# Head norms between the projection chunks, side columns as the stationary operand, and one routing pass for both token tiles

## The reference

```python
def mixer_inputs(h, w_in, q_norm, k_norm, rope):          # first block, x and ctx
    qa, ka, va, fb, qc, kc, vc = jnp.split(h @ w_in, points, axis=-1)
    qa = rms_norm(qa.reshape(b, l, 6, 64), q_norm)
    ka = rms_norm(ka.reshape(b, l, 2, 64), k_norm)
    if rope is not None:                                  # only for x
        qa, ka, qc, kc = (apply_rope(v, cos, sin) for v in (qa, ka, qc, kc))
...
# even layer: h @ ev_w_in has 3072 columns in twelve chunks and 8 more, dt, one for each head
# odd layer: q (8 heads), ksl and kwn (2 heads each) get rms_norm and rope, and then NSA
# experts:
logits = t @ router                                       # 256 x 8
top_val, top_idx = lax.top_k(logits, 2)
gates = sum(one_hot(top_idx) * softmax(top_val))
```

## Time and profile before

| | us |
|---|---|
| median of 3 runs | 2687.01 (2672.03, 2687.01 and 2688.66) |
| profiled execution | 2674.17 |
| its span | 2671.4 |
| PE busy | 2401.7 |
| DVE busy | 1760.9 |
| ACT busy | 1321.8 |
| POOL busy | 201.2 |

### The profile page before, as it was taken

How to read it: one execution, slowest core, us unless ns; L and a number is a source line. 1 busy time by engine, 2 the same in 40 slices (tenths; PEclk the granted TensorE clock), 3 DMA queues, 4 the chain that set the end, 5 groups by cost and what they waited for, 6 DMA issues and landing times. The chain is left out here.

```text
span 2671.4 us, 44765 instructions
## 1 busy us (share of the span) xinstructions
PE 2401.7 (90%) x17271; PEld 2182.7 (82%) x17271; DVE 1760.9 (66%) x2845; ACT 1321.8 (49%) x2069; POOL 201.2 (8%) x200
## 2 busy tenths in 40 slices
PE   7888999889986989979789986676999999999998
PEld 5777898679876879979689986466999999999997
DVE  3645555555555555565555553656999999999997
ACT  2343443434342544432344441224777777777776
POOL 0500000000005000007100005000000000000000
PEclk9988999989998989989689997887999999999999
DMA  8614555155633045534035541023999999999995
GB/s 340 235 50 174 190 214 205 67 208 219 232 134 111 17 163 190 185 119 142 1 121 187 190 185 66 1 87 136 354 346 334 334 345 340 330 346 337 331 351 212
DMA packets 82228, 542.86 MB, mean 203 GB/s; under 512 B 9328, under 2 KB 9840, under 8 KB 33904
## 3 DMA queue, kind: packets, MB, share of 16 engines
q1 hardware_dynamic: 79184, 529.57, 53.4%
q10 hardware_dynamic: 2848, 10.55, 1.1%
HBM read 539.03 MB, written 1.05 MB: 202 GB/s over the span
## 5 line engine op out<-in xcount | busy, mean ns | idle before, releaser
L847 PE MATMUL bank<-w_hi,src_hi 128*128 128x256 f32 x2304 | 657.3, 285 | 14.2 <-DVE src_lo L618 4.6
L2922 DVE TENSOR_TENSOR w_lo<-ring,w_hi 128x1024 fp32r<-128x1024 f32 x528 | 636.7, 1221 | 44.9 <-ACT w_hi L2851 32.8
L848 PE MATMUL bank<-w_lo,src_hi 128*128 128x256 f32 x2304 | 650.6, 282 | 0.0
L849 PE MATMUL bank<-w_hi,src_lo 128*128 128x256 f32 x2304 | 649.2, 282 | 0.0
L847 PEld LDWEIGHTS bank<-w_hi,src_hi 128*128 128x128 f32 x2304 | 438.7, 190 | 32.2 <-issue 23.7
L848 PEld LDWEIGHTS bank<-w_lo,src_hi 128*128 128x128 f32 x2304 | 439.1, 191 | 6.8
L849 PEld LDWEIGHTS bank<-w_hi,src_lo 128*128 128x128 f32 x2304 | 440.0, 191 | 0.0
L847 PE MATMUL bank<-src_hi,w_hi 128*128 128x256 f32 x1472 | 427.2, 290 | 12.7 <-DVE w_lo L1154 8.9
L1154 DVE TENSOR_TENSOR w_lo<-ring,w_hi 128x1024 fp32r<-128x1024 f32 x264 | 322.9, 1223 | 170.1 <-ACT w_hi L1091 170.0
L848 PE MATMUL bank<-src_lo,w_hi 128*128 128x256 f32 x1472 | 422.2, 287 | 0.0
L849 PE MATMUL bank<-src_hi,w_lo 128*128 128x256 f32 x1472 | 421.9, 287 | 0.0
(11 more groups left out here) (410 smaller groups left out, 2837.7 us busy)
## 6 DMA issues: line engine op xcount, KB each, us to landing
ring<-in_moe SPq DMA_DIRECT2D x176, 1024.0 KB, 7.2
ring<-in_ffn SPq DMA_DIRECT2D x66, 1536.0 KB, 6.5
ring<-in_moe SPq DMA_DIRECT2D x176, 512.0 KB, 6.8
ring<-in_ffn_ev SPq DMA_DIRECT2D x22, 1536.0 KB, 6.6
oT<-in_w_ada SPq DMA_DIRECT2D x20, 1024.0 KB, 6.1
big<-in_w_ada SPq DMA_DIRECT2D x20, 1024.0 KB, 8.3
ring<-in_w_in SPq DMA_DIRECT2D x18, 1024.0 KB, 6.7
ring<-in_w_out SPq DMA_DIRECT2D x12, 1024.0 KB, 4.9
```

What stands on the lines that cost most here:

```text
L847: pe.matmul(out, ah, bh, start=start and i == 0, stop=False, skip_group_check=True)
L848: pe.matmul(out, ah, bl, start=False, stop=False, skip_group_check=True)
L849: mm = pe.matmul(out, al, bh, start=False, stop=stop and i == n - 1, skip_group_check=True)
L2922: dve.tensor_tensor(wl, piece, wh.bitcast(F32), ALU.subtract).then_inc(p.w_lo[kind].sem, 1)
```

## The change

- `side_product` swaps its operands: the eight columns are stationary and all 256 tokens stream past, 24 matmuls in place of 48. The result lies on eight partitions; DVE copies it to SBUF (`side_keep`) and PE turns it with two small transposes (`side_turn`). In the even projection the product stands behind chunk 9 of 0 to 11 and the turn behind chunk 10, in banks 6 and 7, so that the chunks have three pairs of banks in place of four.
- First block: POOL norms and turns the A heads of `x` during the projection of `x` itself, when two chunks are taken (and, in layer 0, the small loads have landed). During the context's projection it turns only the C heads (`x_turns1`) and then computes the power for the context's norms.
- `ctx_heads1` has no Block any more. It is `inline`: DVE issues the squares and sums of the context's heads after chunk 1 (chunk 0 in layer 1), and the scaling and gains after the next chunk.
- Odd layer: all norms and turns move from POOL to DVE, between chunks 1 to 5 (`nsa_norms`). POOL keeps the two powers.
- `route` handles both token tiles in each instruction where it can, and releases PE's counting before it computes the weights.

```diff
-def side_product(p, pe):
-
-    for m in range(NT):
-        ms = slice(m * P, m * P + P)
-        mm = products(pe, p.ps[0][:, m * NE:m * NE + NE],
-                      [((p.srcH[:, k, ms], p.srcL[:, k, ms]), (p.sideH[:, k, :], p.sideL[:, k, :]))
-                       for k in range(KT)], True, True)
-    return mm
+def side_product(p, pe, bank):
+
+    mm = products(pe, bank[0:NE, 0:T],
+                  [((p.sideH[:, k, :], p.sideL[:, k, :]), (p.srcH[:, k, :], p.srcL[:, k, :])) for k in range(KT)],
+                  True, True)
+    mm.then_inc(p.sig("side_ready").sem, 1)
+
+
+def side_keep(p, dve, bank):
+
+    dve.wait_ge(*p.sig("side_ready")(1))
+    dve.tensor_copy(p.work[0:NE, 2560:2560 + T], bank[0:NE, 0:T]).then_inc(p.sig("side_kept").sem, 1)
+
+
+def side_turn(p, pe, bank):
+
+    pe.wait_ge(*p.sig("side_kept")(1))
+    for t in range(NT):
+        mm = pe.transpose(bank[:, t * NE:t * NE + NE], p.work[0:NE, 2560 + t * P:2560 + t * P + P], p.ident[0:NE, 0:NE])
+    mm.then_inc(p.sig("side_turned").sem, 1)
...
-    pairs_of_banks = 3 if riders or gate is not None else 4
+    pairs_of_banks = 3 if riders or gate is not None or side is not None else 4
...
+                    if side is not None and c == n - 3:
+                        pe.wait_ge(*sided(1))
+                        side_product(p, pe, p.ps[6])
+                    if side is not None and c == n - 2:
+                        side_turn(p, pe, p.ps[7])
...
-            if side is not None:
-                pe.wait_ge(*taken(n))
-                pe.wait_ge(*sided(1))
-                side_product(p, pe).then_inc(ready.sem, 1)
...
+                if side is not None and c == n - 3:
+                    side_keep(p, dve, p.ps[6])
+                if inline is not None:
+                    inline(dve, chain, c)
...
             if side is not None:
-                dve.wait_ge(*ready(n + 1))
-                dve.tensor_copy(side, p.ps[0][:, 0:NT * NE].rearrange("p (m n) -> p m n", m=NT)).then_inc(taken.sem, 1)
-    ready.passed(total)
-    taken.passed(total)
+                dve.wait_ge(*p.sig("side_turned")(1))
+                dve.tensor_copy(side, p.ps[7][:, 0:NT * NE].rearrange("p (m n) -> p m n", m=NT))
...
-def x_heads1(p, proj, l):
+def square_sums(p, chain, dve, src, junk, st):
+
+    parts, tiles, heads, n = src.shape
+    sq = junk[:, 0:tiles * heads * n].rearrange("p (t h d) -> p t h d", t=tiles, h=heads)
+    chain(dve.tensor_tensor(sq, src, src, ALU.mult))
+    chain(dve.tensor_reduce(st.rearrange("p (t h) -> p t h", t=tiles), sq, AX_X, ALU.add))
+
+
+def mean_squares(p, dve, st, n):
+
+    dve.tensor_scalar(st, st, 1.0 / n, EPS, ALU.mult, ALU.add).then_inc(p.meansq.sem, 1)
+
+
+def scale_heads(chain, dve, src, st):
+
+    parts, tiles, heads, n = src.shape
+    chain(dve.tensor_tensor(src, src, st.rearrange("p (t h) -> p t h", t=tiles).unsqueeze(3)
+                            .broadcast_to([parts, tiles, heads, n]), ALU.mult))
+
+
+def gain_heads(chain, dve, src, gain):
+
+    parts, tiles, heads, n = src.shape
+    chain(dve.tensor_tensor(src, src, gain.unsqueeze(1).unsqueeze(1).broadcast_to([parts, tiles, heads, n]), ALU.mult))
+
+
+def x_heads1(p, proj, l, loads):

     def beside(pool, taken):
         chain, junk = pool_chain(p, pool), p.big[:, 0:2048]
-        norm_rows(p, chain, pool, heads_of(proj, 0, 8), [(0, 6, p.row(ROWS1, "q_norm", l, HD)),
-                                                         (6, 2, p.row(ROWS1, "k_norm", l, HD))], junk, True)
-        for a in (0, 896):
-            rope_rows(chain, pool, heads_of(proj, a, 8), p.con_at(CON1, "rope_c", NT), p.con_at(CON1, "rope_s", NT),
-                      junk)
+        if loads:
+            pool.wait_ge(*p.sig("small_loaded")(16 * len(loads)))
+        pool.wait_ge(*taken(2))
+        src = heads_of(proj, 0, 8)
+        norm_rows(p, chain, pool, src, [(0, 6, p.row(ROWS1, "q_norm", l, HD)), (6, 2, p.row(ROWS1, "k_norm", l, HD))],
+                  junk, True)
+        rope_rows(chain, pool, src, p.con_at(CON1, "rope_c", NT), p.con_at(CON1, "rope_s", NT), junk)
     return beside


+def x_turns1(p, proj, queries):
+
+    def beside(pool, taken):
+        rope_rows(pool_chain(p, pool), pool, heads_of(proj, 896, 8), p.con_at(CON1, "rope_c", NT),
+                  p.con_at(CON1, "rope_s", NT), p.big[:, 0:2048])
+        rsqrts(p, pool, [16 if queries else 4])
+    return beside
+
+
 def ctx_heads1(p, proj, l, queries):

-    gains = [(0, 6, p.row(ROWS1, "q_norm", l, HD)), (6, 2, p.row(ROWS1, "k_norm", l, HD))]
     src = heads_of(proj, 0, 8) if queries else heads_of(proj, 6 * HD, 2)
-    with p.nc.Block(no_gpsimd_drain=True) as block:
-        @block.gpsimd
-        def _(pool):
-            rsqrts(p, pool, [16 if queries else 4])
-
-        @block.vector
-        def _(dve):
...
+    def inline(dve, chain, c):
+        if c == first:
+            square_sums(p, chain, dve, src, p.work[:, 0:1024], st)
+            mean_squares(p, dve, st, HD)
+        if c == first + 1:
+            rsqrt(p, dve, st)
+            scale_heads(chain, dve, src, st)
+            if queries:
+                gain_heads(chain, dve, src[:, :, 0:6, :], p.row(ROWS1, "q_norm", l, HD))
+            gain_heads(chain, dve, src[:, :, src.shape[2] - 2:, :], p.row(ROWS1, "k_norm", l, HD))
+    return inline


...
         linear(p, Normed(x, p.scl[:, 0, 0, :], mod(l, 0, 0)), 6, out=px, loads=second_loads if l == 0 else (),
-               riders=riders(0, (0, 0, 2, 2, 4, 4)) if l == 0 else ())
+               beside=x_heads1(p, px, l, second_loads if l == 0 else ()), riders=riders(0, (0, 0, 2, 2, 4, 4)) if l == 0 else ())
         ctx_src = Normed(ctx, p.scl[:, 0, 1, :], mod(l, 0, 1))
         if l == 0:
-            linear(p, ctx_src, 6, out=pc, beside=x_heads1(p, px, l), riders=riders(6, (0, 0, 2, 2, 4, 4)),
-                   after=norm_scales(p, l, (1,)))
+            linear(p, ctx_src, 6, out=pc, beside=x_turns1(p, px, True), riders=riders(6, (0, 0, 2, 2, 4, 4)),
+                   after=norm_scales(p, l, (1,)), inline=ctx_heads1(p, pc, l, True))
         else:
-            linear(p, ctx_src, 3, out=pc, out_at=[256, 512, 1280], beside=x_heads1(p, px, l))
-        ctx_heads1(p, pc, l, l == 0)
+            linear(p, ctx_src, 3, out=pc, out_at=[256, 512, 1280], beside=x_turns1(p, px, False),
+                   inline=ctx_heads1(p, pc, l, False))
         block1_attention(p, px, l, True)
...
-            norm_rows(p, chain, pool, v, [(0, n, gain)], junk, True)
-            rope_rows(chain, pool, v, p.con_at(CON2, "rope_c", NT), p.con_at(CON2, "rope_s", NT), junk)
+        rsqrts(p, pool, [16, 8])
     return beside
+
+
+def nsa_norms(p):
+
+    queries = heads_of(p.proj, 0, 8)
+    keys = [heads_of(p.proj, 768 + 256 * w, 2) for w in range(2)]
+    st = p.small[:, 0:16]
+    cos, sin = p.con_at(CON2, "rope_c", NT), p.con_at(CON2, "rope_s", NT)
+
+    def inline(dve, chain, c):
+        if c == 1:
+            square_sums(p, chain, dve, queries, p.work[:, 0:1024], st)
+            mean_squares(p, dve, st, HD)
+        if c == 2:
+            rsqrt(p, dve, st)
+            scale_heads(chain, dve, queries, st)
+        if c == 3:
+            gain_heads(chain, dve, queries, p.row(ROWS2, "nsa_q"))
+        if c in (3, 4):
+            square_sums(p, chain, dve, keys[c - 3], p.work[:, 0:256], st[:, 4 * (c - 3):4 * (c - 3) + 4])
+        if c == 4:
+            mean_squares(p, dve, st[:, 0:8], HD)
+            rope_rows(chain, dve, queries, cos, sin, p.work[:, 512:2560])
+        if c == 5:
+            rsqrt(p, dve, st)
+            for w in range(2):
+                scale_heads(chain, dve, keys[w], st[:, 4 * w:4 * w + 4])
+                gain_heads(chain, dve, keys[w], p.row(ROWS2, "nsa_k", 1 + w, HD))
+                rope_rows(chain, dve, keys[w], cos, sin, p.work[:, 512:1024])
+    return inline
...
-            side_product(p, pe).then_inc(logit.sem, 1)
+            side_product(p, pe, p.ps[0])
+            side_turn(p, pe, p.ps[2])
             pe.wait_ge(*chosen(1))
...
-            chain(dve.tensor_copy(logits, p.ps[0][:, 0:16].rearrange("p (t e) -> p t e", t=NT)))
+            side_keep(p, dve, p.ps[0])
+            dve.wait_ge(*p.sig("side_turned")(1))
+            chain(dve.tensor_copy(logits, p.ps[2][:, 0:16].rearrange("p (t e) -> p t e", t=NT)))
             for t in range(NT):
...
+            dve.tensor_tensor(first, lanes, at[:, :, 0:1].broadcast_to([P, NT, NE]), ALU.is_equal)
+            chain(dve.tensor_tensor(second, lanes, at[:, :, 1:2].broadcast_to([P, NT, NE]), ALU.is_equal))
+            dve.tensor_tensor(hot, first, second, ALU.add).then_inc(chosen.sem, 1)
+            dve.wait_ge(*ex(1))
...
-    linear(p, Normed(p.x, p.col("od_mix")), 7, out=p.proj[:, :, 0:O_COLS], beside=nsa_heads(p), loads=[
+    linear(p, Normed(p.x, p.col("od_mix")), 7, out=p.proj[:, :, 0:O_COLS], beside=nsa_heads(p), inline=nsa_norms(p), loads=[
```

74 lines of the change are left out of this document (39 added, 35 removed).

## The result

The changed kernel took **2647.36 us** (median of 4 runs, 2645.13 to 2650.41), the kernel before 2686.99 (2672.03 to 2688.66) on the same chip: a ratio of the means of **0.9865** with a 95% interval of 0.9828 to 0.9903, or some 36 us less (the medians lie 39.6 apart). The forecast was 2640, between 2619 and 2661. A second set of runs gave 0.9864 (2644.27).

What follows compares the result with a forecast made beforehand. TensorE, busy 90% of the span, was taken as the bound, so only its standstills count: 9.0 + 6.9 + 5.0 + 9.9 + 7.8 = 38.6, plus 2 for the clock, 40.6 off the mean 2680.5 gives 2640 us, range 2619 to 2661.

Steps and rivals of the forecast that it cites:

- layer 0, x and context: First block, layer 0: the Block between the context's projection and the attention goes, 9.0 us less (7.5 to 10).
- layer 1, x and context: First block, layer 1: x 3.8 us longer, context to attention 10.7 shorter, together 6.9 us less (6.0 to 7.5).
- even projection: Even layer: side product and turn move between chunks, saving 8.4 us behind them, net 5.0 us less (4.0 to 5.6).
- odd projection: Odd layer's norms on DVE: NSA begins at 1633.3 in place of 1643.2, 9.9 us less (9 to 12).
- route: Router product 3.6 us less, instructions from logits to PE's release 4.3 less; 7.8 in all (6.8 to 9.0).
- Contention: POOL beside x's projection stretches w_lo by 1.1 to 1.6 us, within 3.4 of slack; zero counted, at most 1.5 lost.
- Layer 1's wait: POOL works 26.2 us after chunk 1 of x in layer 1, so the context's front begins 3.8 us later.
- The clock: Shorter holes let PE's clock stay up in some places behind them; 2 us counted.
- Rival 1: The clock stays up behind the shortened holes: gain 46 to 55 us, about 2630 us; chance 0.11.
- Rival 2: Chunks pay through late POOL work beside x and waits at inline norms: gain 18 to 34, about 2655; chance 0.11.
- Rival 3: Savings aren't carried on, as later stages are bound by earlier-issued transfers: gain 8 us, 2672 us; chance 0.05.
- rival 4: POOL locks DVE out in both x projections, w_lo above 4.6 us, PE at half clock: about 2705 us; chance 0.03.

Runs made afterwards that it cites:

- both profiles of before: Two profiles of the unchanged kernel before: the first execution took 2674.17 us, the second 2690.42 us.
- c_turn_waits: The changed kernel with POOL's turn of the C heads waiting until the context's front has split its rows; 2639.24 us, ratio 0.9838.
- route_rows: The changed kernel with the router's 48 matmuls of before and no turn, routing still in one pass; 15.0 us from route's first instruction to the slots.
- warm_fronts: The changed kernel with 32 extra unused matmuls at the start of each norm's front but the first; 2632.69 us, ratio 0.9808.

## Why the prediction was right, and where not

The sum said 40.6 less, measured are 36 (26 to 46 by the interval). The places where TensorE stood still, and most of what each was worth, were right. That the total came so close is in part luck, since terms that were off had opposite signs. Its terms, by the stages above, against both profiles of before:

| | forecast | against the first | against the second |
|---|---|---|---|
| layer 0, x and context | -9.0 | -3.7 | -8.8 |
| layer 1, x and context | -6.9 | -5.2 | -7.5 |
| even projection | -5.0 | -5.2 | -5.6 |
| odd projection | -9.9 | -8.9 | -10.7 |
| route | -7.8 | -10.0 | -9.3 |
| sum | -38.6 | -33.0 | -41.9 |
| NSA and MLA | 0 | +10.7 | +2.6 |

The gap between the two columns is mostly the first chunk of x and of the odd projection. Against the profile with the same first chunk, x in layer 0 is 1.3 us longer, x in layer 1 2.2 longer and the odd projection 10.7 shorter.

**The holes** went as worked out: the Block behind the context, the even product, DVE ending some 4 us behind TensorE in the odd layer (3.1), the weights under the counting. **Contention** was mis-sized in layer 0: "I count zero, since it moves from the context's projection to that of `x`". It does move. The last two copies of x come 1.3 us late by the waits of 0.99 and 0.82 us shown above, within the bound of 1.5, and in the context two like them (0.90 and 0.98 us in the first profile) are gone. But the front of the context isn't in that account. There is no slack in it: the C turn is now the first thing on POOL, and the copy of chunk 0 comes 21.2 us behind the front, where it came after 20.0 before, and 21.0 for 20.0 in layer 1. In layer 1 the last copy is 3.2 us late, which is why the context gained 7.4 us there and not 10.7. With the turn held back (`c_turn_waits`) the stages are 3.8 and 2.8 us shorter. The 3.4 us of slack hold for most `w_lo`, not for `src_lo`.

**Layer 1's wait** was 2.2 us rather than 3.8: POOL needed 24.8 us behind chunk 1, not 26.2. **Route** was under-sized: product -4.3 for -3.6, chain -4.6 for -4.3, and 1.1 for the counting, which I had left alone. `route_rows` brings 1.2 of it back, so it belongs to the product's shape. With it the granted clock is 1.00 behind the product and 0.85 in the counting, and with the 48 narrow matmuls it stays at 0.50.

**NSA and MLA** were put at nothing, and took back 10.7 us against the first profile and 2.6 against the second. No term of the sum stood for the clock inside a stage that the change leaves alone.

**The clock** was to give 2 us. The attention of layer 0 did get shorter, by 1.3; that of layer 1 by 1.5 and the even one by 1.9 against the first profile, by nothing and 0.6 against the second. **Rival 1** came true at one place of three. Behind the shortened holes the attention of layer 1 begins at full clock, with 40 matmuls where there were 20, which the prediction had listed as a sign of being wrong; in layer 0 the clock is 0.72 in the first 4 us and then 0.50, and in the even layer 0.57:

```profile
860.00:866.00 6.00, 5.11 (x40) 3.38 (x36) 3.26 (x5) 3.84 (x7) 0.04 (x1) 1.00 0.00 0
1254.00:1260.00 6.00, 5.77 (x26) 4.18 (x26) 2.40 (x8) 0.18 (x2) 3.65 (x16) 0.57 0.00 0
```

Its gain didn't come: the attention of layer 1 is 89.6 us long with this clock, and 89.6 in the second profile of before, which begins it at 0.50. Filled holes, at other places, gave 12 us (`warm_fronts`).

**Rival 2**'s stalls at inline norms didn't come: at those chunks TensorE waits no longer than the 0.3 us that it waits anyway. Its stretching beside x came, at 1.3 us, and at more in `warm_fronts`. Its sum is also off: 12 to 16 us given back leave a gain of 25 to 29, not 18 to 34. **Rival 3** didn't come: of the 28.7 us by which the slots were early, 28.0 were carried through `moe` to the end. Nor did **rival 4**: the longest `w_lo` beside x was 2.3 us.

**The base.** Taking the mean of the four times, 2680.5, was sound. The first profile of before lies 16 us under its second one, and the gain by the spans is 28 us from the first and 45 from the second, where all runs together say 36.

## What to carry to other kernels

When work moves to another engine, look at what it stands beside in its first few microseconds: the front had no slack here, where the loop behind it had some. A stage-by-stage table of two or more profiles of the same kernel shows what a stage varies by itself, before any difference is explained. And when TensorE waits a few us for a known reason, unused matmuls in the hole can be worth as much as a good reordering: here 12 us, like the whole first-block part of the change.

## What the runs showed of the hardware that I had not expected

- The same instructions of NSA took 112.4, 113.4, 115.3, 119.0, 119.9 and 126.0 us in different kernels, by where the granted clock rose and fell in them. Starting NSA 2.6 us later made it 5.6 us shorter.
- The changed kernel repeated all stages up to the slots within 0.1 us in two profiles, the kernel before differed by up to 5.2 us in one. Why one settles and the other doesn't stays open; two profiles of each are few.
- In the first chunk of layer 0 the first matmul took 0.36 us in the first profile of before, and 0.55 in its second one and in the changed kernel, though nothing ahead of it differs, and the windows from 46 to 50 us give a granted clock of 1.00 for all three, with 19 matmuls in 2 us in the first and 11 or 12 in the others. The granted clock in the records isn't always the rate that the matmuls show.
